# Expert weights with a second place for half of each expert's chunks, in a loop over pairs of experts

## What is computed

```
logits = hf @ w_router + b_router            # 256 tokens, 32 experts
top_vals, top_idx = top_k(logits, 4); gates = softmax(top_vals)
for each expert e, on the rows xb of its tokens:
    gu   = xb @ w_gu[e] + b_gu[e]            # w_gu[e]: 1024 x 2048
    gate = minimum(gu[:, :1024], 7);  up = clip(gu[:, 1024:], -7, 7)
    y    = ((up + 1) * gate * sigmoid(1.702 * gate)) @ w_down[e] + b_down[e]   # w_down[e]: 1024 x 1024
out = sum over a token's four experts of its gate times y
```

## Time and profile before

| | |
|---|---|
| runs | 2381.1, 2372.91, 2378.64 us |
| profiled execution | 2377.8 us, its span 2376.0 us |
| mean granted clock of TensorE | 0.961 |
| TensorE busy | 2163.8 us, 91% of the span, 11564 matmuls |
| VectorE, ScalarE, GpSimd busy | 816.3, 540.1 and 25.3 us |
| DMA | 580.28 MB, mean 244 GB/s |
| w_gu chunks | 256 DMAs of 1024.0 KB, median 17.9 us to landing |
| w_down chunks | 128 DMAs of 1024.0 KB, median 17.6 us to landing |
| L931, the gu products | 519.2 us in 2304 matmuls of 603 ns |
| L982, the dn products | 255.1 us in 1152 matmuls of 595 ns |

### The profile page before, as it was taken

The page is one execution under the profiler, slowest core; times in us unless marked ns, Lnnn a source line. Parts: engine busy times, 40 slices in busy tenths (PEclk is TensorE's granted clock), DMA queues, the critical chain, the costliest instruction groups (busy, mean ns, idle before and its releaser), DMA issues.

```text
span 2376.0 us, 30846 instructions
## 1 busy us (share of the span) xinstructions
PE 2163.8 (91%) x11564; PEld 1367.5 (58%) x11565; DVE 816.3 (34%) x1461; ACT 540.1 (23%) x885; POOL 25.3 (1%) x45
## 2 busy tenths in 40 slices
PE   6967799997999999999999699998999799998999
PEld 2746233332333333333333487777999687777998
DVE  2153122110112211111121237533874147424873
ACT  1131011110111111111111113312553122403652
POOL 0000000000000000000000020000000020000000
PEclk9977899998999999999999899999999899999999
DMA  9642899438999999999899233304544434223533
GB/s 345 213 145 117 334 417 418 200 162 311 393 418 418 417 418 418 418 418 418 342 417 404 80 106 114 135 32 158 189 132 141 125 107 142 107 90 125 187 124 116
DMA packets 219622, 580.28 MB, mean 244 GB/s; under 512 B 22752, under 2 KB 124256, under 8 KB 186624
## 3 DMA queue, kind: packets, MB, share of 16 engines
q1 hardware_dynamic: 219520, 578.83, 64.1%
HBM read 577.48 MB, written 1.31 MB: 244 GB/s over the span
## 4 chain that ended last, share of the span: by engine, by line
PE 73%; DVE 8%; DMA 8%; SPq 5%; issue 3%; ACT 3%; ACTq 0%; DVEq 0%
PE bank L716 21%; PE bank L931 15%; PE bank L982 8%; DMA ring<-in_w_gu 6%; PE bank L1212 3%; PE bank L1214 3%; PE bank L1213 3%; SPq L593 3%; PE bank L894 3%; PE bank L908 3%; DVE heap L1913 2%; SPq L595 2%; PE bank L1228 2%; PE bank L1230 2%; PE bank L1229 2%
## 5 line engine op out<-in xcount | busy, mean ns | idle before, releaser
L931 PE MATMUL bank<-ring,heap 128*64 128x512 f32 x2304 | 519.2, 603 | 18.5 <-DMA ring<-in_w_gu 18.5
L716 PE MATMUL bank<-heap,ring 128*128 128x256 f32 (+2 forms) x2272 | 505.7, 384 | 32.1 <-DVE heap L1858 12.2
L716 PEld LDWEIGHTS bank<-heap,ring 128*128 128x128 f32 (+2 forms) x2272 | 431.3, 191 | 102.7 <-issue 20.2
L931 PEld LDWEIGHTS bank<-ring,heap 128*64 128x64 f32 x2304 | 159.7, 138 | 360.7 <-issue 300.1
L1765 DVE TENSOR_SCALAR heap<-bank 128x256 f32<-128x256 f32 x36 | 15.3, 424 | 763.1 <-PE bank L931 763.1
L982 PE MATMUL bank<-ring,heap 128*64 128x512 f32 x1152 | 255.1, 595 | 0.0
L1212 PE MATMUL bank<-h_hi,w_hi 128*128 128x256 f32 x704 | 201.3, 286 | 18.2 <-DVE h_lo L1981 18.2
L1213 PE MATMUL bank<-h_lo,w_hi 128*128 128x256 f32 x704 | 200.8, 285 | 0.0
L1214 PE MATMUL bank<-h_hi,w_lo 128*128 128x256 f32 x704 | 200.7, 285 | 0.0
L1966 DVE TENSOR_TENSOR w_lo<-ring,w_hi 128x2048 fp32r<-128x2048 f32 (+1 forms) x68 | 151.6, 2229 | 130.2 <-ACT w_hi L1478 130.2
L1478 ACT ACTIVATE w_hi<-ring 128x2048 fp32r<-128x2048 f32 (+1 forms) x68 | 126.6, 1862 | 179.9 <-PE bank L1214 99.6
(11 more groups left out here) (270 smaller groups left out, 1999.1 us busy)
## 6 DMA issues: line engine op xcount, KB each, us to landing
ring<-in_w_gu SPq DMA_DIRECT2D x256, 1024.0 KB, 17.9
ring<-in_w_down SPq DMA_DIRECT2D x128, 1024.0 KB, 17.6
ring<-in_ffn_w_up SPq DMA_DIRECT2D x44, 1024.0 KB, 7.6
ring<-in_w_ada SPq DMA_DIRECT2D x12, 2048.0 KB, 14.5
ring<-in_w_in SPq DMA_DIRECT2D x24, 1024.0 KB, 8.0
ring<-in_ffn_w_down SPq DMA_DIRECT2D x8, 2816.0 KB, 11.4
ring<-in_w_in SPq DMA_DIRECT2D x7, 2048.0 KB, 10.7
ring<-in_w_out SPq DMA_DIRECT2D x6, 2048.0 KB, 14.0
```

The source lines that it names most:

```text
L716: last = mm(outp, w(k), x(k), start=k == 0, stop=k == nk - 1)
L931: last = mm(psum[g][both[f], :], xgT[:, k % 4, k // 4, :], wt[:, g, :, f, :], start=False, stop=k == DT - 1, skip_group_check=True)
```

## The change

The first six chunks of an expert (`TURN` = 6: gu0 to gu5) get a second place in a new area `annex` of 12288 words, right behind the ring (18 places in all, `SLOTS`). Even experts use the ring's places, odd experts the annex's. gu6, gu7 and the four dn chunks keep one place. The place of a chunk is an address in an instruction, so TensorE's and SyncE's loops over experts become loops over pairs whose body is written out for an even and then for an odd expert. VectorE's and ScalarE's loops stay as they are.

A chunk with two places waits for the expert two before it (`last_use`), the others for the expert before, as now. Expert 1's first six chunks are issued once the first gather is done and the bias is ready, since the annex lies over mixer arrays. The first layer's weights in the first six places wait for expert 30 instead of 31.

To make room, the small arrays of the experts start at word 12288 of heap instead of 4672, with `htok` now the first of them. The hidden product is written in place (`act_u` for `hid`), `gateT` shares `x_tok`, and `b_down` and `bias_raw` lie over mixer arrays. `b_down` is therefore loaded later, behind a wait for the mixer's squares (`sqm_ready`), with the bias rows, which now wait for that as well. They are read back twice, into partitions 0 to 63 and 64 to 127 (four DMAs). ScalarE rounds all 128 partitions into one tile `bias_pair`, and VectorE overwrites the upper half with the low part. `bias_sel` picks from both halves by a new constant `eye2`, so that two matmuls over 128 partitions replace the four over 64.

```diff
+SLOTS, TURN = 18, 6
...
+    parts["eye2"] = np.tile(np.eye(HD, HD + 1), (2, 1))
...
         with nc.sbuf_tensor("ring", [P, RING], F32) as ring, nc.sbuf_tensor("heap", [P, HEAP], F32) as heap:
             pass
+        with nc.sbuf_tensor("below_annex", [P, RING], F32),                 nc.sbuf_tensor("annex", [P, SLOTS * UNIT - RING], F32) as annex:
+            pass
...
-        bias_hi, bias_lo = sb("bias_hi", [P, 2, 512], F32R), sb("bias_lo", [P, 2, 512], F32R)
+        sb("below_bias", [P, RING + HEAP - 2 * 320 - 48 - 48 - 128 - 1024 - 39936])
+        bias_pair = sb("bias_pair", [P, 2, 512], F32R)
...
-        exp_stream = Stream(EXPERT, RING)
+        chunk_of = {name: c for c, (name, _) in enumerate(EXPERT)}
+
+        def slot_of(name, odd):
+
+            c = chunk_of[name]
+            return (annex if odd and c < TURN else ring)[:, UNIT * c:UNIT * (c + 1)]
+
+        def arrival_of(name, odd, run):
+
+            sig = exp_in[name, odd if chunk_of[name] < TURN else 0]
+            return sig.sem, sig.at(16, run)
+
+        def last_use(c, e):
+
+            if c < DT - 1:
+                return gu_used.sem, gu_used.at(c + 1, e)
+            if c == DT - 1:
+                return up_full.sem, up_full.at(R, e)
+            if c < len(EXPERT) - 1:
+                return dn_used.sem, dn_used.at(c - DT + 1, e)
+            return y_full.sem, y_full.at(R, e)
...
-        exp_in = {n: signal(f"in_{n}", 16) for n, _ in EXPERT}
+        exp_in = {(n, odd): signal(f"in_{n}_{odd}", 16) for c, (n, _) in enumerate(EXPERT)
+                  for odd in range(2 if c < TURN else 1)}
...
-        b_down = heap[0:NE, 19800:19800 + D]
-        assert take.areas[0][1] <= 19800, take.areas
+        b_down = qT.rearrange("p a b -> p (a b)")[0:NE, :]
+        assert take.areas[0][1] <= 18720, take.areas
         bias_cols = heap[:, 18720:18720 + 512]
-        bias_raw = heap[0:2 * NE, 13720:13720 + 1024].rearrange("p (a b) -> p a b", a=2)
+        bias_raw = xc.rearrange("p a b -> p (a b)").rearrange("p (a b) -> p a b", a=2)
...
-        htok = sq.rearrange("p a b -> p (a b)").rearrange("p (a b) -> p a b", a=TT)
         take_e = Carve()
-        take_e.areas[0][1] = 2 * DT * T + 2 * T + 64
+        take_e.areas[0][1] = SLOTS * UNIT - RING
+        htok = take_e(TT, D)
...
-        hid, hidT, y_sb = take_e(512), take_e(512), take_e(512)
+        hidT, y_sb = take_e(512), take_e(512)
...
-            def load_expert(e, free):
+            def load_chunk(name, e, odd):
                 gu = dram["w_gu"][e].rearrange("(k p) n -> p k n", p=P)
                 dn = dram["w_down"][e].rearrange("(k p) n -> p k n", p=P)
-                for name, _ in EXPERT:
-
-                    sp.wait_ge(*free(name))
-                    j = int(name[2])
-                    if name.startswith("gu"):
-                        sp.dma_start(piece(exp_stream, name, 1)[:, 0, :], gu[:, j, :]).then_inc(exp_in[name].sem, 16)
-                    else:
-                        sp.dma_start(piece(exp_stream, name, 2), dn[:, 2 * j:2 * j + 2, :]).then_inc(exp_in[name].sem, 16)
-
-            def after_mixer(name):
-                lo = exp_stream.at[name]
-                return mix_full.sem, max(MIXFILLS.full(MIX_LAST[m]) for m, w in mixer
-                                         if mix_stream.at[m] < lo + exp_stream.size[name] and mix_stream.at[m] + w > lo)
-
-            def after_expert(e):
-                def free(name):
-                    j = int(name[2])
-                    if name.startswith("gu"):
-                        return (gu_used.sem, gu_used.at(j + 1, e)) if j < DT - 1 else (up_full.sem, up_full.at(R, e))
-                    return (dn_used.sem, dn_used.at(j + 1, e)) if j < 3 else (y_full.sem, y_full.at(R, e))
-                return free
+                j = int(name[2])
+                if name.startswith("gu"):
+                    sp.dma_start(slot_of(name, odd), gu[:, j, :]).then_inc(arrival_of(name, odd, None)[0], 16)
+                else:
+                    sp.dma_start(slot_of(name, odd).rearrange("p (k n) -> p k n", k=2), dn[:, 2 * j:2 * j + 2, :]) \
+                      .then_inc(arrival_of(name, odd, None)[0], 16)
 
 
             sp.wait_ge(bias_sent.sem, 16)
-            sp.wait_ge(mix_full.sem, MIXFILLS.full("o3"))
-            for f in range(2):
-                sp.dma_start(bias_raw[NE * f:NE * (f + 1)].rearrange("e g (c n) -> e (g c) n", n=P),
+            sp.wait_ge(sqm_ready.sem, 2)
+            for g in range(4):
+                f = g % 2
+                sp.dma_start(bias_raw[NE * g:NE * (g + 1)].rearrange("e g (c n) -> e (g c) n", n=P),
                              bias_rows.rearrange("e (b f n) -> f e b n", f=2, n=P)[f]).then_inc(bias_in.sem, 16)
-            load_expert(0, after_mixer)
-            with sp.Fori(0, NE - 1) as e:
-                load_expert(e + 1, after_expert(e))
+            sp.dma_start(b_down, dram["b_down"]).then_inc(bias_in.sem, 16)
+
+            for c, (name, w) in enumerate(EXPERT):
+                sp.wait_ge(mix_full.sem, max(MIXFILLS.full(MIX_LAST[m]) for m, size in mixer
+                                             if mix_stream.at[m] < (c + 1) * w and mix_stream.at[m] + size > c * w))
+                load_chunk(name, 0, 0)
+
+            sp.wait_ge(x_full.sem, R)
+            sp.wait_ge(bias_ready.sem, 1)
+            for c, (name, _) in enumerate(EXPERT):
+                if c >= TURN:
+                    sp.wait_ge(*last_use(c, 0))
+                load_chunk(name, 1, 1)
+            with sp.Fori(0, NE // 2 - 1) as i:
+                for odd in range(2):
+                    for c, (name, _) in enumerate(EXPERT):
+                        sp.wait_ge(*last_use(c, 2 * i + odd + (c >= TURN)))
+                        load_chunk(name, 2 * i + 2 + odd, odd)
...
-                        j = (lay_stream.at[name] + w - 1) // exp_stream.size["gu0"]
-                        if j < DT - 1:
-                            sp.wait_ge(gu_used.sem, gu_used.at(j + 1, NE - 1))
-                        else:
-                            sp.wait_ge(up_full.sem, up_full.at(R, NE - 1))
+                        last = (lay_stream.at[name] + w - 1) // UNIT
+                        sp.wait_ge(*last_use(last, NE - 1 if last >= TURN else NE - 2))
                     else:
 
...
+            pe.wait_ge(bias_in.sem, 5 * 16)
...
                     for g in range(2):
-                        for n, rows in enumerate((bias_hi, bias_lo)):
-                            mm(psum[g], bias_sel[0:2 * NE].rearrange("p a b -> p (a b)"), rows[0:2 * NE, g, :], start=n == 0,
-                               stop=False, skip_group_check=True)
+                        mm(psum[g], bias_sel.rearrange("p a b -> p (a b)"), bias_pair[:, g, :], start=True, stop=False,
+                           skip_group_check=True)
                     for k in range(DT):
                         if r == 0:
-                            pe.wait_ge(exp_in[f"gu{k}"].sem, exp_in[f"gu{k}"].at(16, e))
-                        wt = piece(exp_stream, f"gu{k}", 2).rearrange("p g (c f n) -> p g c f n", f=2, n=P)
+                            pe.wait_ge(*arrival_of(f"gu{k}", odd, run if k < TURN else e))
+                        wt = slot_of(f"gu{k}", odd).rearrange("p (g c f n) -> p g c f n", g=2, f=2, n=P)
                         for g in range(2):
                             for f in range(2):
...
             pe.wait_ge(bias_ready.sem, 1)
-            with pe.Fori(0, NE) as e:
-                n = pe.value_load(counts_i[0:1, bass.ds(e, 1)], min_val=0, max_val=T)
-                with pe.If(n > P):
-                    expert(e, 4)
-                with pe.Else():
-                    with pe.If(n > FEW):
-                        expert(e, 2)
+            with pe.Fori(0, NE // 2) as i:
+                for odd in range(2):
+                    e = 2 * i + odd
+                    n = pe.value_load(counts_i[0:1, bass.ds(e, 1)], min_val=0, max_val=T)
+                    with pe.If(n > P):
+                        expert(e, odd, i, 4)
                     with pe.Else():
-                        expert(e, 1)
+                        with pe.If(n > FEW):
+                            expert(e, odd, i, 2)
+                        with pe.Else():
+                            expert(e, odd, i, 1)
             pe.wait_ge(y_ready.sem, y_ready.at(R, NE))
             combine().then_inc(combined.sem, R)
...
 
-            act.wait_ge(bias_in.sem, 32)
-            f(bias_hi[0:2 * NE], bias_raw, ACT.Copy).then_inc(bias_split.sem, 1)
+            act.wait_ge(bias_in.sem, 5 * 16)
+            f(bias_pair[:, :, :], bias_raw, ACT.Copy).then_inc(bias_split.sem, 1)
             act.wait_ge(slots_ready.sem, 2)
...
                 for f in range(2):
-                    ins = v.tensor_copy(bias_sel[0:2 * NE, f, :],
-                                        const("ident")[0:2 * NE, bass.ds(e + NE * f, 1)].to_broadcast([2 * NE, FEW]))
```

(6 more changed lines are left out.)

## The result

The kernel after takes 2766.73 us (median of 4 runs, 2763.64 to 2771.93), the kernel before 2376.26 us on the same chip (4 runs, 2372.91 to 2381.1). The ratio is 1.1642, 95% interval 1.1621 to 1.1662: 390 us slower. The forecast was 2777 us, in a range of 2540 to 2850.

What follows compares the result with a forecast made beforehand. Before, TensorE's 27.66 us per ordinary expert ran on a lead over weights landing in 30.1 us; after, code fetches would bound it. 447 - 28 - 20 = +399 on 2377.8 us gives 2777 us, range 2540 to 2850.

Steps and rivals of the forecast that it cites:

- The reading of the bound: TensorE's expert loop: the sequencer holds some eight code pieces, drops roughly the longest unused; a missed jump costs some 6 us.
- Step 1: TensorE's expert loop, body written twice: 71 more missed jumps, 77 against 6, adding 447 us.
- Step 2: Weight loads of the experts: the 28 us of waiting go, since a pair outlasts its weights; nothing more can.
- Step 3: Bias matmuls of the experts: each round loses two of four, 0.56 us x 36 rounds, 20 us less.
- Step 4: Bias and b_down loads, splitting instructions, product in place, earlier first-layer weights: no change in time.
- A: TensorE's pair loop: part of the code survives, 34 more misses than now, +171 us, 2549 us; chance 0.29.
- B: Expert loop: code fits, weights decide; six chunks more of lead save 15.1 us; 2366 us, or 2354; chance 0.09.
- C: Expert loop: code fits, second places bring nothing, lead lost in the odd version's cold start; 2370 us; chance 0.04.

## Why the prediction was right

**The reading of the bound.** Seven pieces held, some eight in all, oldest dropped: nine and twelve miss at every jump, and seven and eight do not. Whether the piece fetched longest ago or the one used longest ago is dropped, the runs don't tell apart; on a circle both miss every time. The Trainium skill (Advanced Engine Details and Errata, section ISA Cache) gives TensorE 128 KB in lines of 16 KB, which makes eight. Here the runs agree with that from both sides, with 84 packets at eight touched and 333 at nine. The same section also says "Only 2 cache lines!", which these runs contradict. The two-page window of the Trainium skill (Runtime: NRT & Kernel Launch, section Instruction fetch mechanics) is contradicted too: by it each jump of before over the four-round version would need a fetch, and queue 8 is silent there from 643 us on, with branches of 0.21 us.

**Step 1, the loop over pairs.** 71 more misses were predicted, 77 in all, and 77 branches of 5 us or more are in the trace. The shares were three and two of a pair, as forecast. The forecast for a pair was 87 us, before the bias is taken off; the pair shown takes 86.2, and the ordinary experts 46.5 (even) and 39.0 (odd) on the mean. The gaps were put at 16 and 10 us, and are 17.2 and 9.8. The loss stood with the loop alone (2774 us) and went with another order of the same code (2367 us), so the cause is shown.

**Step 2, six second places.** The 28 us of waiting for weights are recovered, as forecast, but not by the places: with one place each TensorE waits for no DMA either. They go because each pair is now longer than its weights' time.

**Step 3, the bias on one tile.** x72, as forecast. No run changes the bias alone inside the slow loop, and the only pair of kernels there (2788.08 us with the new bias and one place, 2774.35 with the old) goes the other way. The traces show the size all the same. From its first bias matmul to the end of its dn products an ordinary even expert takes 29.43 us in after and 30.03 in the loop over pairs alone, which has the four bias matmuls; an odd one takes 29.35 and 30.26 (means of 13 each). That is 0.6 to 0.9 us less, or 19 to 29 us over 32 experts, against 20 forecast. The times of the kernels hide it because the gaps are 24.7 us longer in after (413.4 against 388.7). Where the code fits, single experts take 0.45 us less, and the kernel 6 us (2362.79 to 2356.73, measured apart, 0.27% between the ratios).

**Step 4, the rest at nothing.** TensorE enters the loop at 236.5 us instead of 240.9; in kernels that differ only behind this point it lies anywhere from 236.3 to 242.5, so no loss is seen. From the last combine on the layers take 1062.8 us instead of 1068.0 (1698.62 and 1308.01 to the span's end), of which 2.3 us are a shorter wait for the split weights. The change's earlier issue of the first layer's weights is not needed for it: the loop over pairs alone, with SyncE's program as before, has 1062.8 us as well, and with the head moved it is 1070.3. So this part varies by some us between kernels that don't differ in it, and its cause is open.

**The sum.** From the loop's entry to the last combine before takes 1067.1 us and after 1462.1: +395.0 against +399 predicted. With -4.4 ahead and -5.2 behind it is +385.4, the two spans' difference. The forecast was 13 us high on the profiled execution and 10 on the median. Taking the 28 us of weights and the 19 to 29 of the bias off again, the misses cost 442 to 452 us in after, against 447.

**What was luck.** So close a hit is better than the reading can promise. The loop over pairs alone has the same 78 long branches, and its misses cost 426 us (+398.1 in the loop, and the 28); it lies 21 us below its forecast. The kernel with one place lies 21 us above its own. The prediction's own range for this case, 2755 to 2859 us, is as wide as these differences; that its middle met the measured time within 10 us is chance, and no run explains the differences.

**The rivals.** A, partial survival, is out: no piece of the circle survives until it is wanted again. B and C would have needed twelve pieces held. B's term for the lead, 15.1 us, was wrong even so: where the code fits, the places bring 0.2 us. C's words on them were nearer: the lead is lost again, though the windows show the other kernel catching up, and not a cold start. That its 2370 us is near what the change measures with the common version first, 2367.61, is chance: that kernel has other jumps.

## What to carry to other kernels

Before a loop's body is written out twice, count the instructions that its commonest path touches, in pieces of some 250, and look whether the instruction queue is silent in the loop and its branches take 0.2 us. Here each jump to a piece that was not held cost some 6 us and a slow restart, and eight pieces were held. Put the common version first and the rare ones behind or inside a rare arm: here that alone turned a loss of 16% into a gain of 0.4%. A second buffer for half the chunks of a stream gave no lead here, where the other half stayed single behind the same queue.

## What the runs showed of the hardware

- Code that no expert runs (2974 us behind the versions, 2380 inside) made the kernel 25% slower when the common path had to jump over it, and nothing slower inside a rare arm.
- The same 78 long branches came with 413.4, 388.7 and 426.4 us of idle TensorE in three kernels (after, the loop over pairs alone, one place for each chunk). The branch to the one-round version lasted 7.4 us in the odd experts of the last two and 4.6 to 5.2 in the even ones behind another one-round expert. Kernels in this state differ by up to 21 us, by a rule that the runs don't settle; moving the loop's head brought 6 and 3 us.
- After a gap of 9.8 us the 64 gu matmuls took 11.76 + 3.60 = 15.4 us, after one of 17.2 us 16.4 us, and without one 13.95: the granted clock in the pair is 0.84, not 1.00, and that part of the loss stands in no wait.
